# Moving the second token tile's first-layer work and two expert-routing steps to other units in a two-layer decoder trunk

## The chip, the cores and the metric

The kernel runs on one core of a Trainium2 chip. The metric is the device time of one execution in microseconds (us). Three runs of the kernel before gave 1695.69, 1697.11 and 1697.17 us; their median is 1697.11 us.

## What is computed

The reference runs 256 tokens of width 1024 through two layers. Each layer adds three things to the residual stream: a mixer, a cross-attention into 256 fixed memory tokens, and a mixture of experts (PEER). Cut to what matters here:

```python
for l in range(2):
    # layer 0: gated linear attention (4 heads) | stick-breaking attention (8 heads)
    # layer 1: block attention (8 heads) | gated linear recurrence
    x = x + mixer(rmsnorm(x), ...)
    x = x + memory_cross_attention(rmsnorm(x), rmsnorm(mem), ...)
    x = x + peer_ffn(rmsnorm(x), wq, subkeys, u, v)

def peer_ffn(...):                     # per token: 8 heads, 16 experts each
    s1, i1 = top_k(q1 @ subkeys1, 16); s2, i2 = top_k(q2 @ subkeys2, 16)
    top_s, eidx = top_k(s1[:, None] + s2[None, :], 16)
    g = softmax(top_s)
    ue, ve = u[eidx], v[eidx]          # rows of 1024 floats each
    return sum(g * gelu(x @ ue) * ve)
```

Every token has its own 128 experts, so each tile of 128 tokens reads 128 times 128 rows of `u` and of `v`. All data is float32.

## The kernel before

Tokens are worked on in two tiles of 128 (t = 0, 1), a token on a partition. One **unit** is one expert of each of the 128 tokens of a tile: GpSimd gathers 128 rows of 2048 floats (u beside v, 1.049 MB) into one of eight slots of `arena` (L2107). VectorE multiplies u with the token's row and sums (L1687). ScalarE makes the gelu, the gain and a 128x128 diagonal matrix of gains in `cst`. TensorE multiplies that diagonal with v in four matmuls of 64x512 and accumulates (psum<-arena,cst). A layer has 256 units: 128 of tile 0, then 128 of tile 1. A slot is free when TensorE is done with its unit, so GpSimd can issue unit u+8 when unit u is through (`taken`, L531).

Everything else is called a front here: the projections, attention, cross-attention and routing that a tile needs before its experts. The front of tile 0 in layer 0 runs alone, in clock steps -108 to 0. The front of tile 1 in layer 0 is written between the units of tile 0, that of layer 1, tile 0, between the units of layer 0, tile 1, and so on. This is an order written out by hand. Each engine's program is a set of Python generators; `until(g)` lets a generator go on only once the clock, which is the number of the unit, has passed g. At each unit every generator of the front is asked for its next piece, so a table of numbers says behind which unit each piece stands on each engine. The tables that matter here are:

```python
FIRST_FROM = (-108, -4)      # clock from which a tile's front in layer 0 counts
LATER_FROM = (PAIRS + 8, 2 * PAIRS + 8)     # the same for layer 1
TAIL_LAG = (4, 6)            # output projection, cross-attention and routing: so much later
PLAN[1] = dict(sq=6, sk=10, ..., sb=16, sb_step=4, gla=2, lv_step=2, go=2, ...)
ROUTE_AT = {unit: (head, step)}             # top-k of heads 2 to 7 of tile 0 on VectorE
GATES_AT = {unit: group}                    # exponentials of their gates on ScalarE
```

The names in `PLAN` are pieces of the mixer in layer 0: `sq`, `sk`, `sv` (queries, keys and values of the stick-breaking attention), `qk`, `gg`, `gv`, `gr` (of the gated linear attention), each one a projection with a weight block of 2 MB (`gg` is small) that stands behind four units, eight matmuls of 128x128 or two of 128x512 to a unit. `sb` and `sb_step` place the rounds of the stick-breaking attention (`breaking`, L727, L1734: scores `zs`, remainders `zr`, output `so`), `gla`, `lv_step` and `go` those of the gated linear attention (`gla`, L774, L1767). The tail (`tail`, L965, L2033) holds the output projection `out01`, the cross-attention, the key projections `pq01` and, on VectorE, twenty routing steps (`route_late`, L1669) two units apart.

For heads 0 and 1 of tile 0 the routing is done before unit 0. For the pairs of heads (2, 3), (4, 5) and (6, 7) it is done by `route_early` (L1697) in four steps each: best keys, best pairs, ranks, and chosen (which writes the indices that GpSimd waits for). Head h is needed from unit 16h on.

The weight blocks of tile 1's front go through two places of 2 MB in `ring`. SyncE issues them in one fixed order, and each waits for the end of the projection that used its place two blocks before (L548). So the place of a projection in the order also sets when the next block but one is fetched:

```python
def load(b):
    name, src, _ = BLOCKS[b]
    s, _, before = PLACE[b]
    if before is not None:
        full(sp, BLOCKS[before][2])
```

The PSUM banks are dealt out in the order in which `first_jobs` (L224) sorts the pieces by the same tables. The fronts of layer 1 hang on `LATER_FROM`, and the memory projections of layer 1 on `MEMORY_FROM = 116`.

Of the kernel before, what the change touches and what calls it, by code (L numbers as in the profile page):

```python
# [60 lines left out]
for _name, _n in (("ident", P), ("ones", P), ("head_ones", P), ("rot", P), ("tri", P),  # L61
# [17 lines left out]
NORM_AHEAD = (0, 9)  # L79
MEMORY_FROM = 116  # L80
LATER_FROM = (PAIRS + 8, 2 * PAIRS + 8)
TAIL_LAG = (4, 6)


PLAN = (dict(sq=6, sk=8, a_unit=2, sv=10, qk=14, gg=18, gate=21, gv=20, gr=24, sb=12, sb_step=4, gla=0, lv_step=2, go=0,
             gv_out=26, gr_out=30),
        dict(sq=6, sk=10, a_unit=1, sv=14, qk=18, gg=22, gate=25, gv=26, gr=32, sb=16, sb_step=4, gla=2, lv_step=2, go=2,
             gv_out=31, gr_out=37))


ROUTE_AT = {1: (2, 0), 4: (2, 1), 7: (2, 2), 10: (2, 3), 13: (4, 0), 17: (6, 0), 21: (4, 1), 24: (6, 1), 44: (4, 2),
            46: (4, 3), 48: (6, 2), 50: (6, 3)}
GATES_AT = {9: 2, 46: 3, 50: 4}
GATES_LAG = 3
LATER_RING = 3
FRONT_BANKS = 4
# [6 lines left out]
def tail_from(l, t):  # L103

    return LATER_FROM[t] if l else FIRST_FROM[t] + TAIL_LAG[t]

# [117 lines left out]
def first_jobs(t):  # L224
# [9 lines left out]
    if t == 0:  # L234
        slots += [(24, 3, "norm_mem"), (28, 3, "xk0.0"), (30, 3, "xk0.1"), (36, 3, "xkn0.0"), (36, 3, "xkn0.1"), (42, 3, "xv0.0"),
                  (57, 3, "xv0.1")]
        slots += [(FIRST_FROM[n] - NORM_AHEAD[n] + 1 - FIRST_FROM[0], 5 * n, f"mean_ev.{n}") for n in range(TT)]
    slots += [(s + TAIL_LAG[t], 4, n) for s, n in tail_jobs(0, t)]
    return [n for _, _, n in sorted(slots, key=lambda x: x[:2])]
# [51 lines left out]
def trunk(nc, d, out_d):  # L291
# [9 lines left out]
    with ExitStack() as ctx:  # L301
# [794 lines left out]
        def _(act):  # L1096
# [57 lines left out]
            def exponentials(first, n, of):  # L1154

                act.wait_ge(top_ready, of + 1)
                fn(top[:, first:first + n, :], top[:, first:first + n, :], ACT.Exp).then_inc(top_exp, 1)
# [15 lines left out]
            def experts(l, t, fronts, closed):  # L1173

                for k in range(PAIRS):
                    u = t * PAIRS + k
                    r = u % SLOTS
                    if l == t == 0 and k in GATES_AT:
                        exponentials(*EARLY_HEADS[GATES_AT[k]], GATES_AT[k])
                    act.wait_ge(dotted, l * UNITS + u + 1)  # L1180
# [324 lines left out]
        def _(dve):  # L1505
# [203 lines left out]
            def experts(l, t, fronts, closed):  # L1709
                for k in range(PAIRS):  # L1710
                    unit(l, t * PAIRS + k)
                    if l == t == 0 and k - GATES_LAG in GATES_AT:
                        of = GATES_AT[k - GATES_LAG]
                        softmax(0, *EARLY_HEADS[of], of)
                    if l == t == 0 and k in ROUTE_AT:
                        route_early(ROUTE_AT[k][0], 2, ROUTE_AT[k][1])
                    if closed and closed[-1][0] == 0 and k == BACK_LAG + 4:
# [474 lines left out]
```

## Time and profile before

| | us |
|---|---|
| median of three runs | 1697.11 |
| the profiled execution's own time | 1697.11 |
| its span in the profile | 1695.0 |
| TensorE busy | 1351.9 (80%) |
| VectorE busy | 996.5 (59%) |
| ScalarE busy | 727.0 (43%) |
| GpSimd busy | 628.1 (37%) |
| moved by the DMA engines | 667.97 MB, 394 GB/s over the span |

The span is 2.1 us shorter than the execution's time; that part lies around the profile. Of the bytes, 536.90 MB are the 512 gathers and 129.52 MB the weights and other inputs. The page cuts the span into 40 slices of 42.4 us and gives for each the busy share of every engine in tenths, TensorE's granted clock in tenths of full speed, the busy share of the 16 DMA engines and the GB/s that they moved. The shares over the whole span say little here: the kernel starts with 180 us in which no expert is gathered, and the rest is a pipeline of 512 units.

### The profile page before, as it was taken

The numbers are of one execution on the slowest core, as the hardware profiler recorded it, in microseconds if no ns is written. First come the engines' busy times: TensorE is split into PE (matmuls) and PEld (weight loads), VectorE is DVE, ScalarE is ACT, GpSimd is POOL, SyncE is SP. The second block draws the span as 40 slices with busy tenths as digits, with TensorE's granted clock in tenths as the row PEclk, the third lists the DMA queues.
The fourth block names the chain that finished last, engine by engine and source line by source line (L and its number), as shares of the span: only waits on it lengthen the run. The fifth ranks groups of instructions, "written<-read, shape, count | busy, mean of one in ns | idle before, by whom it ended". The sixth has DMA issues, their size and how long they took to land.

```text
span 1695.0 us, 24158 instructions
## 1 busy us (share of the span) xinstructions
PE 1351.9 (80%) x8598; PEld 696.0 (41%) x8598; DVE 996.5 (59%) x2529; ACT 727.0 (43%) x2000; POOL 628.1 (37%) x516
## 2 busy tenths in 40 slices
PE   8998899887895896878789567878789667766776
PEld 6776855553461324435356123445356111111110
DVE  0351867774557964474555896584556984444544
ACT  2232247554533453563543344564543443333333
POOL 0000142433432452343332344234343446655663
PEclk9998999988997997998799778989799776676666
DMA  9516899999999999999999999999999999999997
GB/s 384 212 56 229 325 391 414 416 416 422 422 423 421 421 422 423 423 411 422 421 421 423 421 421 421 418 406 421 421 422 421 421 421 422 420 422 420 421 421 305
DMA packets 87193, 667.97 MB, mean 394 GB/s; under 512 B 9616, under 2 KB 12064, under 8 KB 14112
## 3 DMA queue, kind: packets, MB, share of 16 engines
q0 software_dynamic: 73728, 536.90, 76.5%
q1 hardware_dynamic: 13344, 129.52, 18.7%
q8 instruction: 68, 1.11, 0.3%
q14 instruction: 53, 0.43, 0.1%
HBM read 665.33 MB, written 1.05 MB: 393 GB/s over the span
## 4 chain that ended last, share of the span: by engine, by line
PE 39%; DMA 33%; DVE 13%; ACT 7%; issue 5%; POOL 2%; SPq 0%; POOLq 0%; DVEq 0%; PEldq 0%; ACTq 0%
PE psum L608 38%; DMA arena<-in_experts,idxT 33%; DVE arena L1687 6%; POOL arena L2107 2%; ACT L1111 2%; ACT ring L1111 1%; ACT cst L1111 1%; ACT gains L1111 1%; ACT sqb L1111 1%; ACT gelus L1111 1%; DMA ring<-in_ev_sq 1%; DVE red L1655 1%; DVE cst L1647 0%; ACT L1116 0%; DVE rstd L1578 0%
## 5 line engine op out<-in xcount | busy, mean ns | idle before, releaser
L2107 POOL DMA_INDIRECT arena<-in_experts,idxT x512 | 627.9, 1226 | 1045.6 <-PE psum L608 784.5
L608 PE MATMUL psum<-arena,cst 64*64 64x512 f32 (+1 forms) x4102 | 691.5, 761 | 276.3 <-ACT cst L1111 273.3
L1687 DVE CUSTOM_DVE_ANT_0 arena<-arena,xrow 128x1024 f32<-128x1024 f32 x512 | 622.2, 1222 | 485.2 <-DMA arena<-in_experts,idxT 474.6
L608 PEld LDWEIGHTS psum<-arena,cst 64*64 64x64 f32 (+1 forms) x4102 | 130.1, 154 | 675.4 <-ACT cst L1111 594.9
L1111 ACT ACTIVATE gelus<-red 128x1 f32<-128x1 f32 x512 | 103.3, 202 | 707.9 <-DVE red L1687 701.5
L608 PEld LDWEIGHTS psum<-hT,ring 128*128 128x128 f32 x2304 | 277.1, 197 | 114.6 <-issue 108.8
L608 PE MATMUL psum<-hT,ring 128*128 128x128 f32 x2304 | 299.3, 286 | 21.5 <-DVE hT L1530 18.0
L1111 ACT ACTIVATE cst<-cst,gains 128x128 f32<-128x128 f32 x512 | 206.4, 403 | 21.1 <-PE psum L608 4.4
L1111 ACT ACTIVATE gains<-gelus,gateT 128x1 f32<-128x1 f32 x512 | 150.8, 295 | 17.0
L1111 ACT ACT_TABLE_LOAD x66 | 84.7, 1283 | 1.2
L608 PEld LDWEIGHTS psum<-mixT,ring 128*128 128x128 f32 (+1 forms) x592 | 70.6, 194 | 28.2 <-issue 25.7
L608 PE MATMUL psum<-mixT,ring 128*128 128x128 f32 (+1 forms) x592 | 77.4, 284 | 4.8 <-issue 4.1
L1111 ACT ACTIVATE ring<-psum 128x512 f32<-128x512 f32 (+1 forms) x65 | 37.0, 573 | 81.1 <-PE psum L608 60.2
L608 PE MATMUL psum<-ring 128*128 128x128 f32 (+1 forms) x360 | 50.8, 294 | 3.1 <-DVE ring L1786 2.3
L608 PEld LDWEIGHTS psum<-ring 128*128 128x128 f32 (+1 forms) x360 | 44.7, 201 | 18.8 <-issue 12.0
L608 PE MATMUL psum<-ring,hT 128*128 128x512 f32 x96 | 46.4, 613 | 0.0
L1687 DVE DVE_READ_ACCUMULATOR2_ANT red<- 128x1 f32 x512 | 41.8, 82 | 0.0
L1530 DVE SCALAR_TENSOR_TENSOR hT<-xT,vecs,rstdh 128x128 f32<-128x128 f32 x96 | 26.2, 345 | 23.0 <-ACT rstdh L1111 21.7
L608 PE MATMUL psum<-sqb,cst 128*128 128x128 f32 (+1 forms) x176 | 32.8, 337 | 5.3 <-ACT sqb L1111 5.3
L608 PEld LDWEIGHTS psum<-sqb,cst 128*128 128x128 f32 x176 | 24.1, 210 | 18.4 <-issue 9.7
L608 PE MATMUL psum<-hT,cst 128*128 128x128 f32 (+1 forms) x104 | 25.2, 370 | 6.9 <-DMA vecs<-in_vecs 6.9
L1536 DVE TENSOR_TENSOR xT<-xT,psum 128x512 f32<-128x512 f32 x16 | 11.0, 685 | 33.0 <-PE psum L608 24.5
(229 smaller groups left out, 877.2 us busy)
## 6 DMA issues: line engine op xcount, KB each, us to landing
ring<-in_pq SPq DMA_DIRECT2D x15, 2048.0 KB, 9.9
ring<-in_ev_out SPq DMA_DIRECT2D x4, 2048.0 KB
ring<-in_xq SPq DMA_DIRECT2D x4, 2048.0 KB
ring<-in_xo SPq DMA_DIRECT2D x4, 2048.0 KB
arena<-in_experts,idxT POOLq DMA_INDIRECT x512
ring<-in_od_out SPq DMA_DIRECT2D x4, 2048.0 KB
ring<-in_ev_sq SPq DMA_DIRECT2D x2, 2048.0 KB
ring<-in_ev_sk SPq DMA_DIRECT2D x2, 2048.0 KB
```

What stands on the lines that cost most here:

```text
L608: return nc.tensor.matmul(out, lhsT, rhs, start=start, stop=stop)
L1111: return nc.scalar.activation(out, in_, f, **k)
L1530: V.scalar_tensor_tensor(hh[:, c, :], half(xT, t)[:, c, :], gain[:, c:c + 1], rstdh[:], ALU.mult, ALU.mult)\
L1536: V.tensor_tensor(x2, x2, heads_of(o), ALU.add).then_inc(bank_free(name), 1)
L1655: link(V.tensor_reduce(eidx[:, cols], h_.rearrange("p (n c) j -> p n (c j)", c=2), X, ALU.add))
L1687: V.tensor_tensor_reduce(out=ut, in0=ut, in1=xrow[:, u // PAIRS, :], scale=1.0, scalar=0.0, op0=ALU.mult, op1=ALU.add, accum_out=dots[:, k ...
L2107: nc.gpsimd.indirect_dma_start(slot[slot_of(u)], None, d["experts"], bass.IndirectOffsetOnAxis(ap=idxT[:, u:u + 1], axis=0))\
```

## The change

Only numbers in the tables change. `PLAN[1]` spreads the front of tile 1 in layer 0: after each projection comes one unit more, the rounds of the stick-breaking attention are five units apart and not four, the levels of the linear attention three and not two. The tail of tile 1 starts ten units later. In `ROUTE_AT` the four steps of heads 4 and 5 stand behind units 12, 18, 23 and 25 (13, 21, 44 and 46 before), those of heads 6 and 7 behind 14, 20, 53 and 55 (17, 24, 48 and 50 before). `PLAN[0]`, `LATER_FROM` and `MEMORY_FROM` stay.

```diff
-TAIL_LAG = (4, 6)
+TAIL_LAG = (4, 16)
...
-        dict(sq=6, sk=10, a_unit=1, sv=14, qk=18, gg=22, gate=25, gv=26, gr=32, sb=16, sb_step=4, gla=2, lv_step=2, go=2,
-             gv_out=31, gr_out=37))
+        dict(sq=6, sk=11, a_unit=1, sv=16, qk=21, gg=26, gate=29, gv=31, gr=37, sb=17, sb_step=5, gla=6, lv_step=3, go=12,
+             gv_out=36, gr_out=42))
...
-ROUTE_AT = {1: (2, 0), 4: (2, 1), 7: (2, 2), 10: (2, 3), 13: (4, 0), 17: (6, 0), 21: (4, 1), 24: (6, 1), 44: (4, 2),
-            46: (4, 3), 48: (6, 2), 50: (6, 3)}
-GATES_AT = {9: 2, 46: 3, 50: 4}
+ROUTE_AT = {1: (2, 0), 4: (2, 1), 7: (2, 2), 10: (2, 3), 12: (4, 0), 14: (6, 0), 18: (4, 1), 20: (6, 1), 23: (4, 2),
+            25: (4, 3), 53: (6, 2), 55: (6, 3)}
+GATES_AT = {9: 2, 25: 3, 55: 4}
```

The instructions of TensorE and VectorE are the same in number; ScalarE has two table loads more (91 for 89). The order on SyncE and on GpSimd is the same.

On TensorE, behind units 8 to 12, where the keys `sk` end, the values `sv` begin and the first scores stand, before (arena,cst is a unit, hT,ring and ring,hT are projections, ring,xrow and ring alone the scores):

```order
L608 MATMUL psum<-arena,cst 64x512 x4
L608 MATMUL psum<-hT,ring 128x128 x8
L608 MATMUL psum<-arena,cst 64x512 x4
L608 MATMUL psum<-ring,hT 128x512 x2
L608 MATMUL psum<-arena,cst 64x512 x4
L608 MATMUL psum<-ring,hT 128x512 x2
L608 MATMUL psum<-arena,cst 64x512 x4
L608 MATMUL psum<-ring,hT 128x512 x2
L608 MATMUL psum<-ring,xrow 128x128
L608 MATMUL psum<-ring 128x128
```

and now, where the row with x8 is two units with nothing between them:

```order
L608 MATMUL psum<-arena,cst 64x512 x4
L608 MATMUL psum<-hT,ring 128x128 x8
L608 MATMUL psum<-arena,cst 64x512 x8
L608 MATMUL psum<-ring,hT 128x512 x2
L608 MATMUL psum<-arena,cst 64x512 x4
L608 MATMUL psum<-ring,hT 128x512 x2
L608 MATMUL psum<-ring,xrow 128x128
L608 MATMUL psum<-ring 128x128
L608 MATMUL psum<-ring,xrow 128x128
L608 MATMUL psum<-ring 128x128
```

A bare unit stands between the two projections, and everything behind it is later by as much.

On VectorE, from the end of the best keys of heads 4 and 5 to the start of those of heads 6 and 7, before (L1687 is a unit in two instructions, L1749 and L1751 belong to the stick-breaking attention):

```order
L1578 MAX_INDEX rstd<-sqb,ring 128x8 x4
L1687 ISA arena,red<-arena,xrow 128x1024
L1687 ISA red 128x1
L1687 ISA arena,red<-arena,xrow 128x1024
L1687 ISA red 128x1
L1749 SCALAR_TENSOR_TENSOR hT<-psum,hT 128x512
L1751 SCALAR_TENSOR_TENSOR hT<-hT,cst 128x512
L1687 ISA arena,red<-arena,xrow 128x1024
L1687 ISA red 128x1
L1687 ISA arena,red<-arena,xrow 128x1024
L1687 ISA red 128x1
L1563 MAX sqb<-ring 128x8 x4
```

and now:

```order
L1578 MAX_INDEX rstd<-sqb,ring 128x8 x4
L1687 ISA arena,red<-arena,xrow 128x1024
L1687 ISA red 128x1
L1687 ISA arena,red<-arena,xrow 128x1024
L1687 ISA red 128x1
L1563 MAX sqb<-ring 128x8 x4
```

The two steps of eleven rows each stand two units apart and no longer four.

## Rows read from the trace of the kernel before

**Rows 1.** The page's slices of 42.4 us: TensorE, its granted clock, the DMA.

```profile
PE   8998899887895896878789567878789667766776
PEclk9998999988997997998799778989799776676666
DMA  9516899999999999999999999999999999999997
GB/s 384 212 56 229 325 391 414 416 416 422 422 423 421 421 422 423 423 411 422 421 421 423 421 421 421 418 406 421 421 422 421 421 421 422 420 422 420 421 421 305
```

**Rows 2.** Windows: from:to, length, busy us of each engine, PEclk, DMA share, GB/s.

```profile
180.00:220.00 40.00, 36.08 (x301) 31.39 (x300) 36.56 (x170) 14.15 (x39) 12.90 (x11) 0.96 0.92 362
220.00:290.00 70.00, 70.00 (x462) 41.43 (x462) 47.58 (x167) 40.57 (x89) 22.65 (x20) 1.00 1.01 417
290.00:320.00 30.00, 29.88 (x216) 18.98 (x219) 18.22 (x41) 22.84 (x55) 9.95 (x9) 1.00 0.99 404
320.00:400.00 80.00, 68.37 (x506) 40.69 (x506) 59.22 (x135) 38.22 (x102) 35.43 (x29) 0.91 1.01 420
400.00:450.00 50.00, 35.00 (x216) 17.77 (x217) 24.80 (x41) 27.00 (x73) 17.04 (x16) 0.83 1.01 421
...
530.00:600.00 70.00, 54.00 (x280) 19.60 (x280) 65.89 (x214) 34.31 (x92) 32.34 (x26) 0.85 1.01 422
...
1400.00:1680.00 280.00, 198.51 (x900) 31.35 (x904) 139.03 (x225) 100.81 (x336) 163.63 (x110) 0.63 1.01 421
1680.00:1695.00 15.00, 8.01 (x40) 1.12 (x32) 4.99 (x9) 4.20 (x13) 0.00 (x0) 0.73 0.24 95
```

**Rows 3.** The page's DMA queues and its two groups of the gathered units.

```profile
q0 software_dynamic: 73728, 536.90, 76.5%
q1 hardware_dynamic: 13344, 129.52, 18.7%
...
L2107 POOL DMA_INDIRECT arena<-in_experts,idxT x512 | 627.9, 1226 | 1045.6 <-PE psum L608 784.5
...
L1687 DVE CUSTOM_DVE_ANT_0 arena<-arena,xrow 128x1024 f32<-128x1024 f32 x512 | 622.2, 1222 | 485.2 <-DMA arena<-in_experts,idxT 474.6
```

**Rows 4.** Timeline of GpSimd at the ninth gather: start, us, instruction, idle before.

```profile
212.95 1.52 POOL L2107 DMA_INDIRECT arena<-in_experts,idxT  x1 [13.02 <-PE psum L608]
```

**Rows 5.** Timeline of TensorE between two units, two projections (two records a matmul).

```profile
233.37 1.09 PE L608 MATMUL psum<-arena,cst 64*64 64x512 f32 x8
234.39 2.05 PE L608 MATMUL psum<-hT,ring 128*128 128x128 f32 x16
236.37 1.09 PE L608 MATMUL psum<-arena,cst 64*64 64x512 f32 x8
```

**Rows 6.** Timeline of SyncE's issues of three weight blocks.

```profile
249.29 0.33 SPq L552 DMA_DIRECT2D ring<-in_ev_gv  x1
265.96 0.33 SPq L552 DMA_DIRECT2D ring<-in_ev_gr  x1
295.83 0.33 SPq L552 DMA_DIRECT2D ring<-in_ev_out  x1
```

**Rows 7.** Waits in 220 to 320 us: us in total, times, longest.

```profile
POOL arena L2107 <- PE psum L608: 68.4, 27, 6.6
...
DVE arena L1687 <- DMA arena<-in_experts,idxT: 18.6, 10, 4.9
```

**Rows 8.** L1687 alone in 195 to 305 us (two records a unit).

```profile
195.00:305.00 110.00, 37.54 (x63) 0.98 0.99 408
```

**Rows 9.** Timeline of VectorE: first and last row of one step of best keys.

```profile
254.22 0.87 DVE L1563 MAX8 sqb<-ring 128x8 f32<-128x128 f32 x4
...
259.11 0.28 DVE L1578 FIND_INDEX8 rstd<-sqb,ring 128x8 uint32<-128x128 f32 x1
```

**Rows 10.** Group of the adding back of a tile's result on VectorE: busy, mean ns, idle.

```profile
L1694 DVE TENSOR_TENSOR xT<-xT,psum 128x512 f32<-128x512 f32 x4 | 2.6, 679 | 0.0
```

**Rows 11.** The page's group of ScalarE's table loads.

```profile
L1111 ACT ACT_TABLE_LOAD x66 | 84.7, 1283 | 1.2
```

## The prediction

> **What bounds the kernel now.** I read the slices first, then windows around the moved work, then the timelines of the engines in it. The reader is to see in the slices [rows 1] that from the seventh slice (254 us) to the last but one the DMA engines are busy for nine tenths or more and move 406 to 423 GB/s, in most slices 421. TensorE in the same slices goes up and down between five and nine tenths. A busy share that varies beside a rate that doesn't says that the rate is the bound. The windows [rows 2] say it more sharply. In 1400 to 1680 us no front is left, VectorE is half idle, and the DMA moves 421 GB/s. In 400 to 450 us, inside the moved front, it is 421 too, and in 530 to 600 us, where VectorE is busy for 65.89 of 70 us, it is 422. Three very different loads on the engines give one rate. So I take 421 GB/s as the ceiling. A unit is 1.049 MB (536.90 MB over 512 gathers [rows 3]) and costs 2.49 us of it; a weight block of 2.097 MB costs 4.98 us.
>
> From this the time is a sum. Up to 220 us the kernel fills; from there to 1680 us it is bytes over 421 GB/s plus the places where the rate falls short; then 15 us drain the last units at 95 GB/s [rows 2]. The change neither adds nor removes a byte: the 666 MB of gathers and inputs [rows 3] stay. It can only fill or open places where the DMA idles.
>
> Where are they? By the windows [rows 2], the loss is length times the shortfall over 421: 180 to 220 us, 40 x 59/421 = 5.6 us; 220 to 290 us, 70 x 4/421 = 0.7 us; 290 to 320 us, 30 x 17/421 = 1.2 us; 320 to 400 us, 0.2 us; then nothing to 600 us. The 5.6 us come from before the moved instructions: the ninth gather waits 13.02 us for TensorE to finish unit 0 [rows 4], which stands behind tile 0's own front. The first moved piece on TensorE is the keys' projection, behind unit 7 and no longer unit 6, and on VectorE a step behind unit 12. So what the change can win in its own reach is 0.7 + 1.2 + 0.2 = 2.1 us, 0.12% of the time. The low slices further on (411, 406) belong to the fronts of layer 1, whose numbers stay.
>
> **The change, part by part.** *The spread projections.* Between 220 and 290 us TensorE is busy for all 70 us [rows 2], and GpSimd waits 68.4 of the 100 us to 320 us for it, while VectorE waits only 18.6 us for gathered rows [rows 7]. So TensorE sets the pace of the units here and the DMA is full nevertheless, because weight blocks ride along. A unit with eight projection matmuls takes 3.00 us on TensorE (233.37 to 236.37), of which the unit itself is 1.0 (233.37 to 234.39) [rows 5]; four of them are 12.0 us, and the DMA needs 4 x 2.49 + 4.98 = 14.9 us. With one bare unit more it is 13.0 us against 17.4 us. The cover grows, and since 12.0 was already under 14.9, nothing is gained beyond the 0.7 us of that window; I count 0.3.
>
> *The middle, where scores stand beside projections.* The block for gr is issued when the qk projection ends (behind unit 17 then), the next one when gv ends (unit 25) [rows 6]: 8 units in 29.87 us. The DMA could bring 8 units and a block in 8 x 2.49 + 4.98 = 24.9 us. TensorE is late by 5.0 us; most is drawn from the eight slots gathered ahead, the rest is the dip of 1.2 us in 290 to 320 us. Now the same two ends lie behind units 20 and 30, with the same pieces between them and two bare units: 29.87 + 2 x 1.0 = 31.9 us against 10 x 2.49 + 4.98 = 29.9 us. TensorE is late by 2.0 us in place of 5.0, and the slots cover 8 x 2.49 = 19.9 us at best. In proportion the dip falls from 1.2 to 0.5 us; it may vanish. I count a gain of 0.9 with a range from 0.7 to 1.2.
>
> *Over the whole front.* The 31 units 0 to 30, with six blocks issued beside them, take some 109 us (63 records, 31.5 units, in 110 us [rows 8]). The same pieces now lie beside the 36 units 0 to 35: 109 + 5 x 1.0 = 114 us of TensorE against 36 x 2.49 + 6 x 4.98 = 119.5 us of DMA, where before it was 109 against 31 x 2.49 + 6 x 4.98 = 107.1 us. TensorE goes from just late to just early. That looks like much, yet the bytes are the same ones: a front that needs fewer microseconds per unit does not bring the 512th unit sooner when the DMA was at 417 GB/s of 421 already.
>
> *Routing of heads 4 to 7 on VectorE.* A step of best keys lasts 5.2 us (254.22 to 259.39 [rows 9]). Two of them now stand two units apart: 2 x 5.2 + 3 x 1.2 = 14.0 us for units 12 to 14 (1.2 us a unit [rows 3]), against 3 x 2.49 = 7.5 us of DMA and half a block, 2.5 us; VectorE falls back by some 4 us, which the 19.9 us of slots take. In exchange two steps leave units 44 to 46, where nothing was short. Lower bound 0, upper bound the 4 us; I take 0, since 530 to 600 us shows VectorE at 94% with no loss [rows 2].
>
> *The tail ten units later.* Its twenty routing steps stood behind units 89 to 127 and stand behind 99 to 137 now. There they meet the adding back of tile 0's result (two instructions of 0.68 us [rows 10]) and the norm of the memory keys (two of the same size in elements, 128x512), so 4 x 0.68 = 2.7 us more for VectorE within twelve units. The indices of tile 1's first unit come behind unit 115, and its slot is free only after unit 120: VectorE works in order, so the list is there first, by five units where it was fifteen. Two weight blocks for layer 1's first projections, which came behind the routing steps, now fall into the same stretch, so the DMA has 10 us more to do in it and VectorE is less of a limit. I count 0, bounds -0.5 and +2.7 us.
>
> *Two table loads more* on ScalarE: 2 x 1.28 = 2.6 us [rows 11]. ScalarE is busy 40.57 of 70 us [rows 2]; cover is there, cost 0; without it a unit's chain is later by 2.6 us once, which the slots take too.
>
> Sum: -0.3 - 0.9 + 0 + 0 + 0 = -1.2 us. The profiled execution took 1695.0 us of span and 2.1 us around it, 1697.1 us, which is also the median of the runs. I forecast 1697.1 - 1.2 = **1695.9 us**, and call this no change: about 0.2%, 3.4 us, is what a measurement of this kernel can tell from none. Its own range is 1694.0 to 1698.5 us.
>
> **Rivals.**
>
> *Faster: the ceiling is higher than 421.* If TensorE's pace in 195 to 305 us were the limit and the DMA merely happened to stand near its own, the excess would come back: the front was late by 5.0 us in its middle and is late by 2.0 now, the 2.1 us of dips are gone, and a little of the 5.6 us before moves too: 3.0 + 2.1 + 0.5 = 5.6 us, so 1691.5 us. For it: 70 of 70 us busy, and the waits of GpSimd. Against: 421 in the gather-only stretch, where no engine is short, and the DMA share of 1.01. The Trainium skill, "DMA: Bandwidth & Descriptors", section "Where 436 GB/s comes from", gives 435 GB/s as the ceiling of the fabric and says that for reads from HBM a limit near 358 binds; the trace has 421 for 280 us [rows 2], so the lower figure does not hold here, and by the higher one the shortfall of 220 to 400 us (416 GB/s on average) would be 180 x 19/435, an estimate of 8 us by that page.
>
> *Slower: TensorE's clock falls.* The change puts bare units into a stretch in which TensorE never paused, at a granted clock of 1.00, the level of 2.4 GHz [rows 2]. Where TensorE is busy for 35 of 50 us the clock is 0.83 on average, in 530 to 600 us 0.85, in the stretch without fronts 0.63 [rows 2], so part of the time at 1.2 GHz. At 0.85 the 114 us beside units 0 to 35 become 134 us against 119.5 us of DMA; TensorE is late by 14.6 us. If the slots hide as large a part as before (5.0 us late cost 1.2) that costs 3.5 us, if they hide no more than 5 us it costs 9.6; I take 5, so 1702 us. It decides below a mean clock of about 0.9 in 220 to 320 us. Against it: TensorE stays behind its unit waits in the middle part, 31.9 against 29.9 us, so it still has next to no pause. The Trainium skill, "TensorE: Matmul & The Clock Gate", section "HAM oscillation — how this bites in real kernels", speaks against the change: a TensorE that waits for transfers between short bursts of matmuls falls back to the slow clock and starts each burst there. By that rule the projections of units 0 to 16, by now 13.0 us of work in 17.4, would run partly slow.
>
> *Slower: VectorE's bunches are not covered.* Units 12 to 14 cost 4 us and the crossing into tile 1 2.7 us: 1697.1 + 6.7 - 1.2 = 1702.6 us. It decides when VectorE is behind by more than the slots hold, near 20 us. For it speaks that the bunch follows on a stretch (180 to 220 us) in which VectorE is busy for 36.56 of 40 us; against it that 65.89 of 70 us in 530 to 600 us go with 422 GB/s [rows 2].
>
> **How the numbers follow.** No change by the DMA's ceiling 0.66; faster by the higher ceiling 0.13; slower by the clock 0.11; slower by VectorE's bunches 0.10. Of the first I put 0.02 on gains just over 3.4 us. Faster by over 0.2% is then 0.15, within 0.2% 0.64, slower 0.21. The range goes from 1692.5, most of the way to the faster rival, to 1701.0 us, short of the slower ones, and leaves out about 2 in 10.
>
> **What would show it.** In the profile after: 421 GB/s from 320 to 700 us as before; 290 to 320 us above 404; 180 to 220 us again near 362; the ninth gather at 213 us again. gr's block issued about 18 us later than 265.96, the next one some 32 us after it. The clock in 220 to 290 us at 0.95 or more, with TensorE busy for less than 70 us. VectorE at nine tenths or more in the stretch around 560 to 630 us, later by ten units. I am wrong if the rate after 220 us differs from 421 by more than the dips named, on either side, or if a gather waits for its indices.

## Result: 0.54% slower, and the profile after

| | before | after |
|---|---|---|
| median us (range, runs) | 1696.77 (1695.63 to 1697.17, 5) | 1706.52 (1704.41 to 1709.07, 5) |
| profiled execution, span | 1697.11, 1695.0 | 1706.78, 1705.0 |

The ratio is 1.0054, with a 95% interval of 1.0041 to 1.0067: slower, and 5.5 us above the upper end of the range. The page's slices after, beside [rows 1]:

```profile
PE   7997999978689797978689567979689666676776
PEclk9999998899799798989789778989789676666666
DMA  9516799899999999999999999999999999999997
GB/s 380 212 50 246 322 390 414 313 418 421 421 421 423 421 413 423 422 422 421 421 422 422 421 419 421 420 412 416 421 421 421 421 421 421 421 421 421 421 421 309
```

One slice stands out, the eighth (298 to 341 us): 313 GB/s where it was 416. The windows after, columns as in [rows 2]:

```profile
180.00:220.00 40.00, 36.26 (x303) 31.55 (x302) 36.28 (x168) 14.04 (x40) 12.52 (x12) 0.96 0.92 366
220.00:290.00 70.00, 66.77 (x423) 38.94 (x421) 48.82 (x174) 32.74 (x76) 21.29 (x20) 0.90 1.00 410
290.00:320.00 30.00, 26.23 (x109) 12.44 (x106) 15.83 (x35) 21.16 (x39) 7.07 (x7) 0.77 0.73 276
320.00:400.00 80.00, 62.14 (x458) 34.81 (x462) 55.61 (x119) 45.80 (x124) 29.97 (x28) 0.94 1.01 416
400.00:450.00 50.00, 40.54 (x306) 23.06 (x298) 20.30 (x38) 19.56 (x52) 19.22 (x17) 0.94 1.01 421
1400.00:1680.00 280.00, 195.93 (x904) 31.28 (x904) 138.47 (x225) 101.15 (x337) 165.56 (x113) 0.65 1.01 421
```

By the prediction's own measure, length times the shortfall from 421, the three windows from 220 to 400 us lose 1.8 + 10.3 + 1.0 = 13.1 us where they lost 2.1. With 0.4 us less lost in 180 to 220 us the change costs 10.6 us by this sum; the two profiled executions differ by 9.7. Later hardly anything is lost or won back: VectorE multiplies unit 304 at 1148.4 us, where it did at 1138.0.

What happened at 290 us. ScalarE, which now has the gates of heads 4 and 5 behind unit 25 (the `sqb` row; start, us, instruction, idle before):

```profile
286.69 1.28 ACT L1111 ACT_TABLE_LOAD   x1
287.99 0.23 ACT L1111 ACTIVATE sqb<-sqb 128x32 f32<-128x32 f32 x1
288.24 1.28 ACT L1111 ACT_TABLE_LOAD   x1
...
290.51 1.28 ACT L1116 ACT_TABLE_LOAD   x1
291.81 0.60 ACT L1111 ACTIVATE mixT<-psum 128x512 f32<-128x512 f32 x1
...
292.92 0.63 ACT L1111 ACTIVATE hT<-hT 128x512 f32<-128x512 f32 x1
```

VectorE, which waits for it with the remainders of the third round (L1751), and behind them the next unit:

```profile
292.44 0.69 DVE L1756 SCALAR_TENSOR_TENSOR mixT<-mixT,cst 128x512 f32<-128x512 f32 x1 [5.67 <-ACT mixT L1111]
294.31 0.69 DVE L1749 SCALAR_TENSOR_TENSOR hT<-psum,hT 128x512 f32<-128x512 f32 x1 [1.19 <-ACT hT L1111]
295.04 0.69 DVE L1751 SCALAR_TENSOR_TENSOR hT<-hT,cst 128x512 f32<-128x512 f32 x1
```

TensorE, from the last unit ahead of that round to the one behind it:

```profile
290.92 1.09 PE L608 MATMUL psum<-arena,cst 64*64 64x512 f32 x8
295.79 1.22 PE L608 MATMUL psum<-hT,cst 128*128 128x128 f32 x4 [3.77 <-DVE hT L1751]
296.94 0.79 PE L608 MATMUL psum<-ring,xrow 64*128 64x128 f32 x2
...
304.32 1.99 PE L608 MATMUL psum<-arena,cst 64*64 64x512 f32 x8
306.24 2.79 PE L608 MATMUL psum<-ring,hT 128*128 128x512 f32 x4
```

and the same round before:

```profile
284.08 0.61 PE L608 MATMUL psum<-hT,cst 128*128 128x128 f32 x4
284.62 0.49 PE L608 MATMUL psum<-ring,xrow 64*128 64x128 f32 x2
...
288.78 1.09 PE L608 MATMUL psum<-arena,cst 64*64 64x512 f32 x8
```

TensorE stands for 3.77 us. Behind that it runs at its lower level, 1.2 GHz (granted clock 0.50 from 296 to 304 us): a pair of 0.49 us lasts 0.79, the round takes 8.53 us (295.79 to 304.32) where it took 4.70. The Trainium skill, "TensorE: Matmul & The Clock Gate", section "HAM oscillation — how this bites in real kernels", says of a TensorE that waits for transfers between short bursts of matmuls that it falls back to the slow clock and starts each burst there; the trace agrees, here behind a wait for VectorE. From 292.01 to 304.32 us no unit is done, so no slot comes free, and GpSimd stands:

```profile
292.84 1.10 POOL L2107 DMA_INDIRECT arena<-in_experts,idxT  x1 [0.34 <-issue]
307.14 0.94 POOL L2107 DMA_INDIRECT arena<-in_experts,idxT  x1 [13.20 <-PE psum L608]
```

I call such a length from the end of one unit on TensorE to the start of the next a **stretch**: 12.3 us here, and none over 6.5 in 220 to 345 us before. A smaller one of 8.1 us stands at the first round, where TensorE waits 1.93 us up to 256.19 us and its clock falls too. SyncE's issues after, beside [rows 6]:

```profile
253.27 0.33 SPq L552 DMA_DIRECT2D ring<-in_ev_gv  x1
277.72 0.33 SPq L552 DMA_DIRECT2D ring<-in_ev_gr  x1
318.95 0.33 SPq L552 DMA_DIRECT2D ring<-in_ev_out  x1
```

From gr to the next block it is 41.2 us, not the 31.9 forecast. The 9.3 us too many are all on TensorE: the wait 3.77, the round at half clock 3.83 (8.53 - 4.70), the unit behind it 0.90 (1.92 - 1.02) and the projection 0.8 (2.72 - 1.92), the last three from start to start.

### The profile page after: what moved, and what is told of

Read it like the earlier page. It is cut to its first block, busy times and chain, and to the rows that moved or that the text cites. A ratio compares the mean times of both kernels' runs of the same rounds, so it can differ in the third digit from the quotient of the medians.

```text
span 1705.0 us, 24162 instructions
## 1 busy us (share of the span) xinstructions
PE 1364.0 (80%) x8598; PEld 702.1 (41%) x8598; DVE 996.4 (58%) x2529; ACT 729.4 (43%) x2002; POOL 619.0 (36%) x516
## 4 chain that ended last, share of the span: by engine, by line
PE 37%; DMA 34%; DVE 12%; ACT 8%; issue 5%; POOL 3%; SPq 0%; POOLq 0%; DVEq 0%; PEldq 0%; ACTq 0%
PE psum L608 36%; DMA arena<-in_experts,idxT 33%; DVE arena L1687 6%; POOL arena L2107 3%; ACT L1111 2%; ACT ring L1111 1%; ACT cst L1111 1%; ACT gains L1111 1%; ACT sqb L1111 1%; ACT gelus L1111 1%; DMA ring<-in_ev_sq 1%; ACT L1116 1%; DVE red L1655 0%; DVE cst L1647 0%; PE psum L1005 0%
## 5 line engine op out<-in xcount | busy, mean ns | idle before, releaser
L2107 POOL DMA_INDIRECT arena<-in_experts,idxT x512 | 618.8, 1209 | 1065.0 <-PE psum L608 808.1
L1687 DVE CUSTOM_DVE_ANT_0 arena<-arena,xrow 128x1024 f32<-128x1024 f32 x512 | 621.9, 1222 | 466.4 <-DMA arena<-in_experts,idxT 465.9
L608 PEld LDWEIGHTS psum<-hT,ring 128*128 128x128 f32 x2304 | 281.6, 200 | 123.6 <-issue 116.8
L608 PE MATMUL psum<-hT,ring 128*128 128x128 f32 x2304 | 304.0, 289 | 27.1 <-DVE hT L1530 22.7
L608 PEld LDWEIGHTS psum<-ring 128*128 128x128 f32 (+1 forms) x360 | 42.9, 196 | 16.9 <-issue 13.1
L1687 DVE DVE_READ_ACCUMULATOR2_ANT red<- 128x1 f32 x512 | 42.0, 82 | 0.0
L608 PE MATMUL psum<-hT,cst 128*128 128x128 f32 (+1 forms) x104 | 28.8, 410 | 12.0 <-DMA vecs<-in_vecs 6.3
L1536 DVE TENSOR_TENSOR xT<-xT,psum 128x512 f32<-128x512 f32 x16 | 10.9, 684 | 32.9 <-PE psum L608 32.9
## 6 DMA issues: line engine op xcount, KB each, us to landing
ring<-in_xo SPq DMA_DIRECT2D x4, 2048.0 KB, 11.8
```

The source lines that it names most:

```text
L608: return nc.tensor.matmul(out, lhsT, rhs, start=start, stop=stop)
L1536: V.tensor_tensor(x2, x2, heads_of(o), ALU.add).then_inc(bank_free(name), 1)
L1687: V.tensor_tensor_reduce(out=ut, in0=ut, in1=xrow[:, u // PAIRS, :], scale=1.0, scalar=0.0, op0=ALU.mult, op1=ALU.add, accum_out=dots[:, k ...
L2107: nc.gpsimd.indirect_dma_start(slot[slot_of(u)], None, d["experts"], bass.IndirectOffsetOnAxis(ap=idxT[:, u:u + 1], axis=0))\
```

## The experiments

Each kernel was timed beside the kernel before. "Stretch" is the longest ones in 220 to 400 us of its trace (before has one of 7.8 at 350 us), "rate" the GB/s over the same window. Both are read from one execution, and "traced" is that execution's own time: e10's is its fastest, almost 6 us under its median, e11's its slowest, almost 4 us above. So stretch and rate go with the traced time, and the verdict goes with the ratio.

| kernel | stretch us | rate | traced us | median us (runs) | ratio, 95% |
|---|---|---|---|---|---|
| before | 7.8 | 416 | 1697.1 | 1696.4 to 1697.7 | 1 |
| after | 8.1, 12.3 | 390 | 1706.8 | 1706.5 (5) | 1.0054, 1.0041 to 1.0067 |
| e1 routing and gates alone | 9.1, 8.4 | 408 | 1699.6 | 1701.0 (8) | 1.0027, 1.0017 to 1.0038 |
| e2 plan and tail alone | 10.3 | 404 | 1700.9 | 1700.9 (8) | 1.0024, 1.0013 to 1.0034 |
| e5 tail alone | under 7 | 418 | 1696.4 | 1697.0 (11) | 1.0005, 0.9996 to 1.0014 |
| e3 after, gates later | 8.5 | 403 | 1702.7 | 1700.5 (11) | 1.0022, 1.0013 to 1.0031 |
| e7 routing alone | 7.6, 9.4 | 403 | 1703.0 | 1700.4 (11) | 1.0015, 1.0007 to 1.0024 |
| e18 four routing steps alone | 7.8 | 415 | 1698.4 | 1696.4 (11) | 0.9999, 0.9990 to 1.0008 |
| e4 after, wait filled | 9.2, 8.7 | 397 | 1705.6 | 1705.0 (5) | 1.0041, 1.0027 to 1.0055 |
| e8 e2, first wait filled | 7.3, 9.2 | 403 | 1701.0 | 1701.0 (11) | 1.0022, 1.0013 to 1.0031 |
| e9 before, a wait put in | 13.9, 7.6 | 386 | 1708.4 | 1709.2 (5) | 1.0073, 1.0060 to 1.0086 |
| e10 e9, the wait filled | 10.9, 7.8 | 402 | 1700.7 | 1706.6 (6) | 1.0057, 1.0040 to 1.0075 |
| e15 work put in at 255 us | 14.1, 7.8 | 397 | 1705.4 | 1705.4 (5) | 1.0049, 1.0035 to 1.0062 |
| e16 the same at 404 us | 7.8; 9.6 at 403 | 414 | 1698.4 | 1696.6 (11) | 0.9999, 0.9990 to 1.0008 |
| e11 e2, routing steps clear | 10.1 | 394 | 1705.8 | 1701.9 (6) | 1.0032, 1.0020 to 1.0044 |
| e12 rounds alone | 14.1, 7.2 | 394 | 1705.7 | 1703.5 (6) | 1.0044, 1.0031 to 1.0057 |
| e13 projections, levels, tail | 7.2, 7.1 | 413 | 1698.7 | 1698.3 (11) | 1.0006, 0.9997 to 1.0015 |
| e14 e12, levels two later | 10.3 | 400 | 1701.6 | 1704.4 (5) | 1.0048, 1.0034 to 1.0062 |
| e17 e14 and the tail later | under 7 | 416 | 1696.7 | 1696.7 (11) | 0.9999, 0.9990 to 1.0008 |
| e19 e2, rounds one earlier | 7.9, 14.0 | 389 | 1706.4 | 1708.1 (5) | 1.0068, 1.0054 to 1.0081 |

**Which half.** e1 is the kernel before with the new `ROUTE_AT` and `GATES_AT`, e2 the changed one with the old ones, e5 the kernel before with

```diff
-TAIL_LAG = (4, 6)
+TAIL_LAG = (4, 16)
```

> The kernel before with the new ROUTE_AT and GATES_AT alone; projections, attention and tail stand where they stood. Theory 1 (the gates' exponentials of heads 4 and 5, with two table loads, stand on ScalarE at unit 25 ahead of a stick-breaking round, TensorE idles for 3.8 us, its clock halves and the eight slots run empty): the exponentials meet another round here (the rounds are four units apart and start one unit earlier, so the softening pieces stand at units 14, 18, 22, 26), so part of the loss, 2 to 8 us: 1699 to 1705 us. Theory 2 (the spread of the projections by itself costs it): 1696 to 1698 us. Theory 3 (VectorE's two steps of best keys at units 12 and 14): nearly the whole loss, 1703 to 1707 us, with the clock down around units 14 to 17.

> The changed kernel with the old ROUTE_AT and GATES_AT: only the spread and the tail ten units later. Theories 1 and 3 (the moved routing costs it): 1695 to 1699 us, no slice under 400 GB/s between 220 and 400 us, TensorE's clock at 0.95 or more in 240 to 300 us. Theory 2 (the spread costs it): 1703 to 1708 us.

> Of the change only the tail of tile 1, ten units later, is put into the kernel before. If my account of 220 to 400 us is whole, the tail is innocent: 1696 to 1698.5 us, a ratio between 0.9995 and 1.001, gv to out1 near 67 us as before, and 421 GB/s in 400 to 700 us. The rival is that a part of the 4 to 5 us that plan and tail cost together belongs to the tail (its bound in the prediction was +2.7 us): then 1699 us or more, with a rate under 418 GB/s somewhere in 540 to 640 us.

Each half costs 0.25%, some 4 us, and the tail nothing. e2 lies between my two ranges, since each theory put the whole loss into one half. It shows how a lighter load per unit costs. Its units and the first round's chain, on VectorE, ScalarE and TensorE:

```profile
247.66 1.23 DVE L1687 CUSTOM_DVE_ANT_0 arena<-arena,xrow 128x1024 f32<-128x1024 f32 x1 [2.43 <-DMA arena<-in_experts,idxT]
...
253.96 0.69 DVE L1751 SCALAR_TENSOR_TENSOR hT<-hT,cst 128x512 f32<-128x512 f32 x1
```

```profile
248.93 0.20 ACT L1111 ACTIVATE gelus<-red 128x1 f32<-128x1 f32 x1 [2.70 <-DVE red L1687]
...
251.84 1.29 ACT L1111 ACTIVATE hT<-hT 128x512 f32<-128x512 f32 x2
```

```profile
254.70 1.22 PE L608 MATMUL psum<-hT,cst 128*128 128x128 f32 x4 [3.67 <-DVE hT L1751]
```

VectorE waits for gathered rows, ScalarE for VectorE's product, and the softening of the round (hT<-hT) stands behind that unit on ScalarE. With a bare unit ahead of the round TensorE has caught up with the transfers, comes to the round before this chain is through, and stands.

**Routing and gates.** e3 is the changed kernel with

```diff
-GATES_AT = {9: 2, 25: 3, 55: 4}
+GATES_AT = {9: 2, 40: 3, 55: 4}
```

e7 is the kernel before with the new `ROUTE_AT` and, of the gates, those of heads 4 and 5 left at 46. e18 is the kernel before with four steps of it:

```diff
-13: (4, 0), 17: (6, 0), 21: (4, 1), 24: (6, 1)
+12: (4, 0), 14: (6, 0), 18: (4, 1), 20: (6, 1)
```

> The changed kernel with the exponentials of heads 4 and 5 behind unit 40 and no longer 25 (the softmax behind 43); everything else as changed. Theory 1: ScalarE is 2.8 us earlier at the third stick-breaking round, TensorE idles about 1 us there in place of 3.8, the hole of 203 GB/s in 300 to 320 us goes: 1696 to 1699 us. Theory 2 or 3: the hole stays, 1704 to 1708 us.

> The kernel before with the new ROUTE_AT, but the exponentials of heads 4 and 5 on ScalarE left behind unit 46. With both tables new and the old plan, the loss was 4.6 us and TensorE idled for 2.19 us at 299 us in the last stick-breaking round. Theory 1 (the exponentials with their two table loads delay that round): 1696 to 1698.5 us, no idle over 1 us on TensorE at that round, the next weight block issued less than 22 us after the one at 295 us. Theory 3 (VectorE's moved steps cost it): 1700 to 1702 us.

> The kernel before with only four routing steps moved, best keys and best pairs of heads 4 to 7 behind units 12, 14, 18 and 20 (13, 17, 21 and 24 before); ranks and choice of heads 4 and 5 stay behind 44 and 46. All routing moved with the gates left cost 2.7 us, with TensorE waiting 1.64 us near 300 us. If the early bunch does that, this costs 2 to 3.5 us, 1699 to 1700.5 us. If the two steps brought forward from 44 and 46 into units 23 and 25 do it, this one costs nothing, 1696.5 to 1698 us.

The gates' place is 5.4 us of the change's 9.7 by the ratios, 6.1 by the medians (e3 against after): in e3 the third round's wait is 0.81 us and the rate from 300 to 320 us is, after and in e3:

```profile
300.00:320.00 20.00, 20.00 (x81) 8.39 (x81) 9.56 (x23) 13.09 (x22) 4.09 (x4) 0.80 0.59 203
```

```profile
300.00:320.00 20.00, 20.00 (x109) 8.77 (x101) 12.14 (x26) 16.21 (x30) 5.10 (x6) 1.00 0.96 375
```

e3 takes as long as e2, so on the new plan the moved routing steps cost nothing beyond the noise; e3 misses the 1696 to 1699 us that I expected, because I had no cost for the plan. On the old plan the gates' move is worth less, 1.0027 against 1.0015, and these intervals meet. e18 shows that the early bunch, the one that I had priced, costs nothing. So the 2.7 us of e7 come from the later steps that it moves as well: ranks and choice of heads 4 and 5 to units 23 and 25, those of heads 6 and 7 to 53 and 55. The second pair is not it: from 340 to 420 us, around it, e7 moves 423 GB/s. From 300 to 330 us it moves 353 where e18 has 418. The steps at 23 and 25 stand on VectorE from 281.79 to 284.5 and 289.08 to 292.5 us, the fourth round's remainders are late, and TensorE waits 1.64 us up to 301.75.

**Wait, clock or length.** e4 and e8 put four matmuls of 128x512, whose result is overwritten, ahead of a wait (e4 in the changed kernel's third round, e8 in e2's first):

```diff
-                        pe.wait_ge(sb_rem, sb_count(t, p))
                         o, done = job(f"zr.{t}.{p}")
+                        if t and p == 2:
+                            for _ in range(4):
+                                mm(o, ident, cst[:, 0:512])
+                        pe.wait_ge(sb_rem, sb_count(t, p))
```

e9 is the kernel before with VectorE's piece of the first round two units later, e10 that with six such matmuls ahead of the wait:

```diff
-                    yield from until(g + 3 + PLAN[t]["sb_step"] * p)
+                    yield from until(g + (5 if t and p == 0 else 3) + PLAN[t]["sb_step"] * p)
```

e15 is the kernel before with ten in the first round (`range(10)`, p == 0), e16 with the same ten ahead of the query norm of the cross-attention (unit 63):

```diff
-                pe.wait_ge(xq_sq, q + 1)
                 o, done = job(f"xqn{e}")
+                if l == 0 and t == 1:
+                    for _ in range(10):
+                        mm(o, ident, cst[:, 0:512])
+                pe.wait_ge(xq_sq, q + 1)
```

> The changed kernel with four matmuls of 128x512 more, in the third stick-breaking round of tile 1, ahead of TensorE's wait for VectorE; they write a bank that the next matmuls overwrite. They fill the idle 3.8 us and change no wait of another engine. If the halved clock is what turns the 3.8 us into the hole: the round's matmuls take 5 us in place of 8.6, two units are 4 to 5 us earlier, and the time falls by 3 to 6 us, to 1701 to 1703 us. If the wait for ScalarE alone makes the hole: 1706 to 1708 us, since the filler gives nothing.

> The spread plan and late tail with the old routing tables, and four matmuls of 128x512 more in the first stick-breaking round of tile 1, ahead of TensorE's wait for VectorE. Without them TensorE idled for 3.67 us at 254.7 us and then ran at half clock; the qk projection ended 27.2 us after the values'. If the halved clock carries the spread's loss: 24 us or less between the two weight issues and 1697 to 1699 us. If the wait and the units themselves carry it: 26 us or more and 1700 to 1702 us.

> The kernel before with one thing changed: VectorE makes the first stick-breaking round's remainders of tile 1 two units later (behind unit 17 and its step of best keys, no longer behind unit 15). TensorE, which never paused in 213 to 320 us, is to wait some 5 to 6 us at 255 us. No bare units, no moved routing. If a wait of TensorE in this stretch is what costs, by itself and by the clock behind it: the issue of gr comes 24 us or more after that of gv (16.7 before), and 1701 to 1706 us. If the eight slots cover such a wait, as the prediction took it: 1696 to 1699 us.

> The same wait as in the kernel with the wait put in, and six matmuls of 128x512 more that TensorE runs while it waits, so that its clock stays up. The difference between the two is the clock's part. If the clock carries half or more of the loss: 2 to 5 us less than with the wait alone. If it is the wait: within 1 us of it.

> The kernel before with ten matmuls more of 128x512, whose result is overwritten, ahead of the remainders of the first round near 255 us: some 8.9 us of work at the full clock between two units, and no wait. With VectorE's remainders two units later in the same place (a wait of 5.32 us and half clock behind it, 13.9 us between two units) the time was 12.5 us longer. If length without a unit is what costs and the idle as such nothing, this one costs about as much per us of length: 8 to 11 us more, 1705 to 1708 us. If the idle and the clock behind it are the cause, and plain work is covered by the slots gathered ahead, it costs 0 to 4 us.

> The same ten matmuls ahead of the cross-attention's query norm near 404 us, where TensorE is busy for only 35 of 50 us. If the slots do cover a stretch of about 9 us wherever TensorE has time left behind it to catch up, this costs nothing: 1696 to 1698 us. If eight slots never cover a stretch of 9 us, because only four to six gathers are on their way when it begins, it costs 2 us or more here as well.

The fillers do what they should to the clock: in e4 the third round lasts 4.7 us again. The time hardly follows: by the medians e4 and e10 lie 1.5 and 2.7 us under the kernels without them, within the intervals, and e8 not at all, its wait having gone to the second round (2.33 us up to 274.68). These runs don't measure the clock's share: e10's own times go from 1700.7 to 1711.0 us, its traced execution is 7.7 us shorter than e9's, and in e4's trace the first round, which has no filler, waits 3.66 us where it waited 1.93. e9 itself, at 1709.2, cost more than the 1701 to 1706 us that I had expected. What decides is seen in the last pair. e15, TensorE and then windows:

```profile
255.01 8.75 PE L608 MATMUL psum<-cst 128*128 128x512 f32 x20
...
267.27 1.09 PE L608 MATMUL psum<-arena,cst 64*64 64x512 f32 x8
```

```profile
255.00:260.00 5.00, 5.00 (x14) 2.29 (x13) 4.16 (x22) 0.90 (x3) 0.00 (x0) 1.00 0.99 419
260.00:265.00 5.00, 5.00 (x18) 2.56 (x16) 4.35 (x17) 1.63 (x4) 0.00 (x0) 1.00 1.01 419
265.00:270.00 5.00, 5.00 (x36) 3.59 (x36) 0.77 (x3) 1.16 (x2) 0.81 (x1) 1.00 0.80 333
270.00:275.00 5.00, 5.00 (x44) 3.39 (x42) 1.48 (x3) 3.41 (x6) 1.06 (x2) 1.00 0.73 231
```

```profile
269.19 0.94 POOL L2110 DMA_INDIRECT arena<-in_experts,idxT  x1 [14.23 <-PE psum L608]
```

e16, the same work 148 us later:

```profile
402.94 8.85 PE L608 MATMUL psum<-cst 128*128 128x512 f32 x20
...
412.58 2.95 PE L608 MATMUL psum<-arena,cst 64*64 64x512 f32 x24
```

```profile
405.00:410.00 5.00, 5.00 (x13) 2.18 (x12) 1.23 (x2) 1.40 (x4) 0.40 (x1) 1.00 1.00 423
410.00:415.00 5.00, 5.00 (x31) 1.59 (x29) 1.23 (x2) 1.50 (x4) 0.50 (x1) 1.00 1.01 415
415.00:420.00 5.00, 2.68 (x14) 1.70 (x7) 2.43 (x4) 4.10 (x7) 2.32 (x3) 0.80 1.02 419
```

At a clock of 1.00 and without any idle, 8.75 us of work cost 8.2 us at 255 us and nothing at 404. At 255 us the slots carry the DMA for some 10 us, until about 265; then it falls to 231 GB/s, and since TensorE is busy for 20 of 20 us in every window up to 320 us, the lead, the units gathered ahead, is not built up again. At 404 us TensorE has three units ready at once behind the stretch (x24 records), frees three slots, and the DMA never falls below 415. e9, with a stretch as long as e15's but made of 5.32 us of wait and a round at half clock, costs 11.6 us by the medians (12.4 by the ratio) against 8.2; idle looks dearer than work of the same length, but the two intervals meet, so this is not shown.

The kernel before has such a wait itself, ahead of the output projection, with the half clock behind it (3.75 us for 2.05) and a stretch of 7.8 us:

```profile
353.89 3.75 PE L608 MATMUL psum<-mixT,ring 128*128 128x128 f32 x16 [4.13 <-issue]
```

```profile
360.00:370.00 10.00, 10.00 (x83) 7.20 (x82) 7.89 (x13) 6.15 (x14) 4.00 (x4) 1.00 1.01 402
```

It costs the DMA half a microsecond. So a wait with the half clock behind it isn't dear as such either. e14 below, where the wait at this same place is 6.66 us and the stretch 10.3, loses far more.

**Which part of the spread.** e12 is the kernel before with one number changed; e14 moves the levels and output of the linear attention too, e17 the tail as well; e13 is e2 with the rounds left where they were, e19 with the first round one unit earlier; e11 is e2 with the routing of heads 4 and 6 moved away from the rounds.

```diff
-sb=16, sb_step=4, gla=2, lv_step=2, go=2      # before
+sb=16, sb_step=5, gla=2, lv_step=2, go=2      # e12
+sb=16, sb_step=5, gla=4, lv_step=2, go=4      # e14, e17 (with TAIL_LAG (4, 16))
-sb=17, sb_step=5, gla=6                       # e2
+sb=16, sb_step=4, gla=6                       # e13
+sb=16, sb_step=5, gla=6                       # e19
-13: (4, 0), 17: (6, 0), 21: (4, 1), 24: (6, 1)
+18: (4, 0), 22: (6, 0), 32: (4, 1), 35: (6, 1)   # e11
```

> The spread plan and the tail of the change, with the gates late as before and with the routing steps of heads 4 and 6 moved clear of the rounds (best keys behind units 18 and 22, best pairs behind 32 and 35). If the spread costs because VectorE's best keys stand just ahead of a round whose scores TensorE waits for, TensorE's wait of 3.67 us at 254.7 us is gone, gv to gr takes 22 us or less in place of 27.2, and the time is 1697 to 1699 us. If the spread itself costs (the bare units let TensorE come to the rounds before VectorE and ScalarE have them ready, whatever stands there), a wait of 2 to 4 us stays in the first rounds and the time is 1700 to 1702 us.

> The kernel before with one number of the plan changed: the rounds of the stick-breaking attention are five units apart and not four, the projections stay where they are. If the spread costs by bare units ahead of the first round, this does nothing to the first round, and TensorE's load per unit falls only behind it: no wait over 1 us, 1696 to 1698 us. If a lighter load per unit anywhere in 250 to 320 us makes TensorE catch up with VectorE's chain, a wait of 2 us or more appears at the second or third round and the time is 1699 to 1701 us.

> The plan and the tail of the change with the routing as before, but the rounds of the stick-breaking attention left at their old places (sb=16, sb_step=4); so only the projections and the linear attention are spread. With the rounds spread as well it was 1700.9 us, with the rounds spread alone 1703.5 us. If the length between two units on TensorE decides (it was 10.3 us with the whole plan, 14.1 us with the rounds alone, 6.4 us before), the time follows it here too: up to 7 us long, 1696 to 1698 us; 10 us, about 1701 us. If a lighter load per unit always costs, whatever the lengths are, it is 1700 to 1702 us with no stretch over 7 us.

> The kernel with the rounds alone five units apart, and in addition the levels and the output of the linear attention two units later, so that the fourth round and the first levels no longer stand between the same two units (there TensorE ran 9.9 us from 309.69 us without a unit, behind a wait of 2.17 us). If that meeting cost the 7 us, the longest stretch without a unit falls from 14.1 to 9 us or less and the time to 1696.5 to 1699.5 us; if the rounds' distance itself costs, it stays at 1702 us or more.

> Rounds five units apart, levels and output of the linear attention two units later, and now the tail ten units later as in the change (alone it cost nothing). Without the tail's shift this cost 8 us in the timings; its profile has no hole left at 300 to 340 us but a new one at 360 us, where TensorE stood 6.66 us ahead of the output projection, which comes right behind the linear attention's output. If it is such meetings of two stages at one unit that cost, the tail's shift takes the second one away and the time is 1695.5 to 1699 us, no stretch without a unit over 8 us. If rounds five units apart cost as such, it stays at 1702 us or more.

> The change's plan and tail with the old routing and gates, and with one number of the plan moved back: the first round at sb=16 and not 17, still five units apart. The whole plan cost 4 us, and TensorE waited 3.67 us for VectorE's remainders of the first round; with the rounds at their old places it cost 1 us and TensorE waited 0.51 us. If the bare unit that stands just ahead of the first round is what makes TensorE come too early, the wait falls under 1.5 us and the time to 1697 to 1699 us. If the distance of five does it, it stays at 1700 to 1702 us.

My theory for e11 fell: the wait at the first round is 3.44 us without any best keys near it. e12 cost more than the whole plan by its median and more than either of my ranges, though its interval and e2's just meet. Its ScalarE and TensorE around the fourth round:

```profile
298.86 3.25 ACT L1111 ACTIVATE ring<-ring 128x256 f32<-128x256 f32 x15
```

```profile
309.69 0.71 PE L608 MATMUL psum<-hT,cst 128*128 128x128 f32 x4 [2.17 <-DVE hT L1751]
...
316.57 1.22 PE L608 MATMUL psum<-ring,mixT 64*128 64x128 f32 x4
...
319.59 1.98 PE L608 MATMUL psum<-arena,cst 64*64 64x512 f32 x8
```

Fifteen exponentials of the linear attention, between two table loads, now stand ahead of this round on ScalarE, and the levels (ring,mixT 64x128) fall between the same two units as the round: 14.1 us without a unit. e14 takes that away, 424 and 403 GB/s in 300 to 320 and 320 to 340 us, but its linear attention now ends just ahead of the output projection, which needs it, and there TensorE stands for 6.66 us:

```profile
358.45 0.69 DVE L1860 SCALAR_TENSOR_TENSOR mixT<-ring 128x512 f32<-128x512 f32 x1
```

```profile
359.24 3.75 PE L608 MATMUL psum<-mixT,ring 128*128 128x128 f32 x16 [6.66 <-issue]
```

The profile names no releaser, but VectorE's last write of the attention's output ends 0.10 us ahead. From 360 to 380 us the DMA moves 244 GB/s; e14 lost there what it won, and I had not foreseen it. With the tail later as well (e17) no stretch is over 7 us and nothing is lost, though the rounds are five units apart. So it is not the distance of the rounds as such. e13, with the bare units and 1.0006, says the same of these. e19 lies above both my ranges: the first round's wait is gone, as expected, but the third now comes 4.30 us too early (at 286.06) and the gate's projection falls into the same stretch, 14.0 us, 1.0068. No version was faster than the kernel before beyond its interval.

## Why the prediction was wrong

- **The ceiling** held: 421 or 422 GB/s from 400 to 700 us in both kernels, in e15 and e16 too, and 421 from 1400 to 1680 us. The fall came from below it.
- **The spread projections** (-0.3): about nothing, 1.0006 in e13, with an interval from 0.9997 that has room for the 0.3. TensorE was to have under 70 us busy in 220 to 290 and a clock of 0.95 or more; it had 66.77, as forecast, and 0.90, which is not.
- **The middle** (-0.9) is the first of two steps that failed, in its words "TensorE is late by 2.0 us in place of 5.0, and the slots cover 8 x 2.49 = 19.9 us at best". It summed TensorE's busy time as if the pieces could be worked off without a pause. The gain in load per unit was real, but TensorE doesn't spend it on units: it comes earlier to a round whose input hangs on VectorE and ScalarE, which hang on the gathered rows. In e2, which has the plan without the routing, it waits 3.67 us and then works at half clock, and in place of a gain of 1.2 us there is a loss of some 4 us. And the cover was mis-sized: 19.9 us is eight slots all on their way; at 255 us it was some 10 us (e15).
- **The routing of heads 4 to 7** (0, "which the 19.9 us of slots take"): the early bunch costs nothing (e18), so the 0 was right for it; the late steps at 23 and 25, which I had not priced at all on VectorE's way to the fourth round, cost 2.7 us on the old plan (e7).
- **The tail** (0): 1.0005 in e5. Right.
- **Two table loads** ("cover is there, cost 0"): the second step that failed and the largest miss, 5.4 to 6.1 us (e3 against after). ScalarE was busy for 40.57 of 70 us, but the loads, with the exponential between them, stand ahead of the one operation that TensorE waits for next. The Trainium skill, "ScalarE: Activation LUTs", section "What ACT_TABLE_LOAD costs", adds a drain of some 1380 ns to each load; in the rows above the exponential starts 0.02 us behind the load's end (286.69 + 1.28, 287.99) and the next load 0.02 us behind the exponential's, so here a load is 1.28 us without a drain and the pair with its exponential 2.84, from 286.69 to 289.53.
- **The rivals.** The clock did fall, to 0.90 and 0.77 in the two windows. But the rival had it as the cause, a gradual slowing below a mean of 0.9; it is the follower of a wait. Filling the wait won 0 to 2.7 us by the medians. The 1702 us of that rival were nearer than the forecast, by another way. VectorE's bunches named the wrong bunch. A wait of TensorE for the remainders was in neither.
- **Signs forecast**: gr was issued 11.8 us later, not 18; the next block 41.2 us behind it, not 32; 290 to 320 us had 276 GB/s, not above 404; 560 to 630 us had VectorE at 86%, not nine tenths, with 415 GB/s. The signs ahead of the moved pieces came true, 366 GB/s from 180 to 220 us and the ninth gather at 212 us, and no gather behind it waited for its indices.

The stretch orders the kernels but is no exact price: e1 and e2, with 9.1 and 10.3 us, cost 4 us more than before, e13 with 7.2 next to nothing. The rate is the price. By the prediction's measure, 180 x (421 - rate)/421 for 220 to 400 us, the loss above before's 2.1 us is 1.3 in e13, 3.4 in e1, 5.1 in e2 and 11.1 after; their traced executions are 1.6, 2.5, 3.8 and 9.7 us longer. In the other fifteen the two agree within 2.4 us. Open is the share of the clock in the 9.7 us, since a filler takes away the half clock but leaves most of the stretch, and what a stretch of a given length will cost at a given place.

## What to carry to other kernels

Where one engine does the pipeline's units and the odd pieces of another stage, don't sum its work over a region: follow, at each piece with an input from another engine, when that input is ready and when the engine now gets there. Lighter load means it gets there earlier and waits. Look for the longest stretch without a unit, compare it with the transfers that are really on their way when it begins, and ask whether the engine has time behind it to refill the slots. A small operation on an engine that is half idle is free only if it doesn't stand just ahead of the one operation that the busy engine waits for next.

## What the runs showed of the hardware

- After a wait of 3.77 us (5.32 in e9, 3.67 in e2) TensorE worked at the 1.2 GHz level for the whole round and the unit behind it, 8.6 to 10.5 us, and for part of the next projection (3.56 us in e2 where 2.05 is usual). Waits of 1.64 (e7), 1.93 (after, first round), 2.17 (e12) and 2.19 us (e1) were followed by that level too, 0.6 to 2.4 us behind their end. After waits of 0.8 us (e3's and e2's third round) and 1.15 (e19's second) it stayed at 2.4 through the round.
- With TensorE at full clock, ten matmuls of 128x512 f32 took 8.75 and 8.85 us, 0.88 us each.
- GpSimd issued nothing for 14.23 us in e15, from 254.96 us on, with the DMA still at 419 GB/s for the first 10 of them.
